# Attention queries and keys computed with tokens on the partitions instead of channels, in a two-layer transformer block on one core

## What is computed

```python
proj = jnp.einsum('bsd,de->bse', x, w_in)          # 2048 -> q, k, v, gate (2048 each), f_logit (16)
q = rms_norm(heads(q), q_gain)                     # 16 heads of 128; mean square over the head's 128
k = rms_norm(heads(k), k_gain)
c = jnp.cumsum(log_sigmoid(f_logit + b_f), axis=1) # per head and token
s = einsum('bhqd,bhkd->bhqk', q, k) * 128 ** -0.5 + c[query] - c[key]
p = softmax(where(key_pos <= q_pos, s, -inf))
y = (p @ v) * silu(gate);   out = y @ w_out
```

## Time and profile before

| | us |
|---|---|
| three runs: lowest, median, highest | 2485.38, 2486.83, 2490.3 |
| the profiled execution: its own time | 2487.29 |
| its span in the profile | 2485.4 |
| TensorE busy | 2411.2 (97%) |
| VectorE busy | 1700.3 (68%) |
| ScalarE busy | 1257.2 (51%) |
| GpSimd busy | 560.0 (23%) |

### The profile page before, as it was taken

How to read it: one execution, slowest core, us unless ns; L and a number is a source line. 1 busy time by engine, 2 the same in 40 slices (tenths; PEclk the granted TensorE clock), 3 DMA queues, 4 the chain that set the end, 5 groups by cost and what they waited for, 6 DMA issues and landing times.

```text
span 2485.4 us, 34202 instructions
## 1 busy us (share of the span) xinstructions
PE 2411.2 (97%) x13500; PEld 2079.5 (84%) x13500; DVE 1700.3 (68%) x2266; ACT 1257.2 (51%) x1780; POOL 560.0 (23%) x540
## 2 busy tenths in 40 slices
PE   7998999999999999999999999997999999999997
PEld 6777878888888888888788888886888888888886
DVE  7897578775566775577775766767666675666676
ACT  6767455444344444465555655635444444444444
POOL 4263154221013231152200000021221210221233
PEclk9999999999999999999999999999999999999998
DMA  7444646665565665556456555554565666555652
GB/s 241 145 135 153 224 153 188 187 191 182 190 198 188 188 188 179 184 170 194 143 158 180 157 170 170 152 172 135 160 190 178 189 181 197 163 189 178 190 178 94
DMA packets 126673, 434.90 MB, mean 175 GB/s; under 512 B 13489, under 2 KB 21041, under 8 KB 126513
## 3 DMA queue, kind: packets, MB, share of 16 engines
q1 hardware_dynamic: 126512, 432.72, 56.3%
HBM read 430.57 MB, written 2.10 MB: 174 GB/s over the span
## 4 chain that ended last, share of the span: by engine, by line
PE 88%; DVE 6%; ACT 3%; POOL 2%; issue 1%; DMA 0%; ACTq 0%; SPq 0%; POOLq 0%; DVEq 0%
PE bank L586 87%; DVE wlo L1251 2%; DVE S L1251 1%; ACT whi L874 1%; POOL hT L1805 1%; POOL acc L1805 1%; DVE hT L1254 1%; DVE ev L1264 0%; DVE ev L1254 0%; DVE S L1254 0%; ACT hT L1182 0%; PE bank L794 0%; ACT L1081 0%; DMA hT<-in_xT 0%; DVE xa L1254 0%
## 5 line engine op out<-in xcount | busy, mean ns | idle before, releaser
L1251 DVE TENSOR_TENSOR wlo<-raw,whi 128x1024 fp32r<-128x1024 f32 (+1 forms) x820 | 1026.0, 1258 | 672.1 <-ACT whi L874 670.1
L586 PE MATMUL bank<-xa,whi 128*128 128x512 f32 (+1 forms) x3968 | 1254.0, 398 | 24.5 <-DVE wlo L1251 11.4
L874 ACT ACTIVATE whi<-raw 128x1024 fp32r<-128x1024 f32 (+1 forms) x822 | 847.3, 1040 | 780.9 <-PE bank L586 775.5
L586 PEld LDWEIGHTS bank<-xa,wlo 128*128 128x128 f32 x3904 | 737.7, 189 | 173.0
L586 PE MATMUL bank<-xa,wlo 128*128 128x256 f32 x3904 | 773.8, 279 | 0.0
L586 PEld LDWEIGHTS bank<-xa,whi 128*128 128x128 f32 x3968 | 609.9, 189 | 39.5 <-DVE wlo L1251 16.1
L586 PE MATMUL bank<-xb,whi 128*128 128x512 f32 (+1 forms) x1948 | 571.4, 378 | 2.4 <-ACT S L1055 2.4
L586 PEld LDWEIGHTS bank<-xb,wlo 128*128 128x128 f32 x1776 | 336.0, 189 | 71.6
L586 PE MATMUL bank<-xb,wlo 128*128 128x256 f32 x1776 | 365.3, 279 | 0.0
L586 PEld LDWEIGHTS bank<-xb,whi 128*128 128x128 f32 x1948 | 300.5, 190 | 3.7 <-issue 3.0
L586 PE MATMUL bank<-whi,xa 128*128 128x512 f32 x768 | 245.0, 401 | 15.1 <-DVE wlo L1251 7.6
(11 more groups left out here) (193 smaller groups left out, 1379.4 us busy)
## 6 DMA issues: line engine op xcount, KB each, us to landing
raw<-in_w SPq DMA_DIRECT2D x792, 512.0 KB, 3.7
raw<-in_w SPq DMA_DIRECT2D x29, 256.0 KB, 2.7
hT<-in_xT SPq DMA_DIRECT2D x4, 512.0 KB, 7.5
hT<-in_xT SPq DMA_DIRECT2D x1, 2048.0 KB, 9.9
out<-hT SPq DMA_DIRECT2D x4, 512.0 KB, 3.0
X<-in_dec SPq DMA_DIRECT2D x8, 192.0 KB, 3.8
con<-in_con SPq DMA_DIRECT2D x1, 768.0 KB, 12.0
hT<-in_rcnt SPq DMA_DIRECT2D x1, 512.0 KB, 5.6
```

The lines of the kernel that those rows point to most:

```text
L586: return pe.matmul(o, w, x, start=start, stop=stop, skip_group_check=True)
L874: act.activation(hi, r, ACT.Copy).then_inc(*w_high(i))
L1251: return dve.tensor_tensor(o, x, y, op)
```

## The change

q and k become natural blocks of 512 columns (four heads at once). Their squares are taken by ScalarE straight from the bank and summed by VectorE along the free axis. After root and reciprocal, VectorE scales the tile while emptying it, four heads in one instruction, into `qkn`; TensorE transposes it to channels on partitions, eight transpositions for q and eight for k per group, and ScalarE copies the result out, k with the gains. `fq_total` and `fk_total` are gone. The forget row is no longer spread into a bank of its own and copied: the same product, now 384 columns wide, is accumulated onto the scores, and `soft` loses two of its four wide instructions. The order of blocks changes to fv, gates(0), fq, fk, gates(2) for the first three groups and fq, gates(0), fk, fv, gates(2) for the last. Heads are scored at e+4, e+5, e+7 and e+8 after the one `fk` block of the group.

The core of the diff (layout, then TensorE, ScalarE, VectorE):

```diff
+        def normed(w, col):
+            e = block(w, g, xa3, "fox_w_in", col + 512 * g, nat, "natural", 512)
+            late(e + 1, w + "_norm", g)
+            late(e + 3, w + "_turn", g)
+            return e
+        def heads(e, attend):
+            for i, (n, late_by) in enumerate(zip((4, 5, 7, 8), attend)):
+                for step in ("scores", "soft", "soft_exp", "soft_scale", "turn_p"):
+                    late(e + n, step, 4 * g + i)
+                    n += 1
+                late(e + n + late_by, "attend", 4 * g + i)
+                late(e + n + late_by + 1, "attend_split", 4 * g + i)
+        if g < 3:
+            values()
...
             gates(0)
+            normed("fq", 0)
+            heads(normed("fk", D), (0, 0, 0, 0))
+        else:
+            normed("fq", 0)
             gates(0)
-        for i in (0, 2):
-            e = block("fq", (g, i), xa3, "fox_w_in", 512 * g + 128 * i, full)
-            late(e + 1, "fq_total", g, i)
-            late(e + 2, "fq_norm", g, i)
-            e = block("fk", (g, i), xa3, "fox_w_in", D + 512 * g + 128 * i, full)
-            late(e + 1, "fk_total", g, i)
-            late(e + 2, "fk_norm", g, i)
...
+            heads(normed("fk", D), (0, 0, 2, 2))
+            values()
+        gates(2)
```

```diff
+                    elif step in ("fq_turn", "fk_turn"):
...
+                        for t in range(2):
+                            q.wait_ge(*vec_evac.of("tile", tile_of[w, g] + t))
+                        for i in range(4):
                             for t in range(2):
-                                m = mm(bank[6 + j][:, t:t + 1], sq[:, j, 128 * t:128 * t + 128], ones[:, 0:1], True, True)
+                                o = 256 * (i % 2) + 128 * t
+                                m = pe.transpose(bank[6 + i // 2][:, o:o + 128], qkn[w][:, t, 128 * i:128 * i + 128], ident)
...
-                            mm(bank[4 + j][:, 0:T], ones, sq[:, j, :], True, True).then_inc(*side("fk_total", g, i + j))
...
-                        mm(bank[6][:, 0:256], hot[:, h:h + 1].broadcast_to((48, 128)), rows[:, 0:256], True,
-                           True).then_inc(*side("forget_row", h))
+                        mm(B[:, 128:384], q_t[i][:, 128:256], k_t[i][:, :], False)
+                        mm(B[:, 0:384], hot[:, h:h + 1].broadcast_to((48, 128)), rows[:, 0:384], False,
+                           True).then_inc(*side("scores", h))
```

```diff
+                    elif step in ("fq", "fk"):
...
+                            act.activation(qk_sq[t], bank[n % 4][:, :], ACT.Square).then_inc(*squares(step, g, t))
+                    elif step in ("fq_norm", "fk_norm"):
...
+                        act.activation(qk_f[w], qk_f[w], ACT.Sqrt, scale=1.0 if w == "fq" else 1.0 / 128,
+                                       bias=eps128 if w == "fq" else eps6).then_inc(*act_val(w + "_norm", g))
+                    elif step in ("fq_turn", "fk_turn"):
...
+                            act.activation(qk_t[w][:, 512 * i:512 * i + 512], bank[6 + i][:, :], ACT.Copy,
+                                           scale=gains if w == "fk" else 1.0).then_inc(*act_evac(w + "_turn", g, i))
```

```diff
+                            dve.tensor_reduce(qk_f[step][:, 4 * t:4 * t + 4],
+                                              qk_sq[t].rearrange("p (h c) -> p h c", h=4), AX,
+                                              ALU.add).then_inc(*vec_val(step + "_sum", g, t))
...
+                            tt(qkn[w][:, t, :].rearrange("p (h c) -> p h c", h=4),
+                               bank[n % 4][:, :].rearrange("p (h c) -> p h c", h=4), f,
+                               ALU.mult).then_inc(*vec_evac("tile", n))
...
-                        stt(p[:, 0:128], B[:, 0:128], f[:, 0:1], r[:, 0:128], ALU.mult,
-                            ALU.add).then_inc(*vec_val("soft_half", h))
-                        stt(p[:, 128:384], B[:, 128:384], f[:, 1:2], r[:, 0:256], ALU.mult,
-                            ALU.add).then_inc(*vec_val("soft_in", h))
```

More of the change, by code:

```diff
@@ L259, in gates, with values @@
             late(e + 1, "fgate_silu", g, i)
-        if g:
-            gates(0)
[L262 to L266, removed]
-            gates(0)
-        if g < 3:
-            gates(2)
-        for i in (0, 2):
-            e = block("fq", (g, i), xa3, "fox_w_in", 512 * g + 128 * i, full)
-            late(e + 1, "fq_total", g, i)
-            late(e + 2, "fq_norm", g, i)
-            e = block("fk", (g, i), xa3, "fox_w_in", D + 512 * g + 128 * i, full)
-            late(e + 1, "fk_total", g, i)
-            late(e + 2, "fk_norm", g, i)
[L277 to L281, removed]
+        def values():
+            block("fv", g, xa3, "fox_w_in", 2 * D + 512 * g, nat, "natural", 512)
+        def normed(w, col):
[12 more added lines that the diff above has]
+            values()
+            if g == 0:
+                e = block("forget", 0, xa3, "fox_w_in", 4 * D, [(0, 16)], "stacked", cols=16)
+                late(e + 1, "forget_turn")
+                late(e + 3, "forget_sums")
+            gates(0)
+            normed("fq", 0)
+            heads(normed("fk", D), (0, 0, 0, 0))
+        else:
+            normed("fq", 0)
+            gates(0)
+            heads(normed("fk", D), (0, 0, 2, 2))
+            values()
+        gates(2)
     ends["fox"] = len(uses) - 1
@@ L791, in tensor_program @@
                         q.wait_ge(*vec_val.of("soft", h))
-                        q.wait_ge(*(act_evac.of("turn_p", h - 1) if h % 4 else act_evac.of("fq_norm", h // 4, 3)))
+                        q.wait_ge(*(act_evac.of("turn_p", h - 1) if h % 4 else act_evac.of("fk_turn", h // 4, 1)))
                         for n in range(3):
@@ L799, in tensor_program @@
                         q.wait_ge(*act_evac.of("turn_p", h))
[L800 to L803, removed]
+                        q.wait_ge(*act_evac.of("tile", tile_of["fv", h // 4] + 1))
+                        q.wait_ge(*(vec_val.of("attended", h - 1) if h % 4 else act_evac.of("fk_turn", h // 4, 0)))
                         mm(bank[6][:, 0:256], v_t[:, 0, c], PT[w][:, 0:256], True)
@@ L1085, in scalar_program @@
                         q.wait_ge(*vec_val.of("forget_row"))
[L1086 to L1112, removed]
-                            q.wait_ge(*side.of("fk_total", g, i + j))
-                            if i:
-                                q.wait_ge(*vec_val.of("fk", g, j))
-                            elif g:
-                                q.wait_ge(*vec_val.of("fk", g - 1, 2 + j))
-                            act.activation(rr[j], bank[4 + j][:, 0:T], ACT.Sqrt, scale=1.0 / 128,
-                                           bias=eps6).then_inc(*act_evac("fk_norm", g, i + j))
-                    elif step == "scores":
-                        h, = k
-                        q.wait_ge(*side.of("forget_row", h))
-                        if h >= 2:
-                            q.wait_ge(*side.of("attend", h - 2))
-                        act.activation(PT[h % 2][:, 0:T], bank[6][:, 0:T], ACT.Copy).then_inc(*act_evac("forget_row", h))
@@ L1166, in scalar_program @@
                             elif i >= KT - 2:
[L1167 removed]
+                                q.wait_ge(*(pool_val.of("ret_square", 7, 2 + j) if l else vec_val.of("fk_sum", 3, 0)))
                                 q.wait_ge(*vec_evac.of("last", l, i))
```

124 lines of the change are left out of this document (65 added, 59 removed).

## The result

| | before | after |
|---|---|---|
| median of five executions, us | 2486.83 | 2474.52 |
| lowest and highest | 2485.38, 2490.3 | 2474.42, 2477.4 |
| span in the profile | 2485.4 | 2472.6 |

The ratio is 0.9951, 95% interval 0.9937 to 0.9966: 12.3 us less, where 10.6 were forecast (2476.2, range 2473 to 2482.5).

What follows compares the result with a forecast made beforehand. The prediction took fox to be bound by TensorE's own instructions; -4.3 - 14.0 + 6.8 + 0.9 = -10.6 us from the median of 2486.83 gave 2476.2, with a range of 2473 to 2482.5.

Steps and rivals of the forecast that it cites:

- The bound: In fox, TensorE's own instructions set the time; work taken from VectorE or ScalarE pays nothing.
- Natural for turned, -4.3: q and k blocks in fox: natural steps of 0.680 replace turned ones of 0.697, 4.3 us less, bounds 0 and -4.3.
- rival 4: q and k blocks: the natural form gains nothing, so the sum is -6.3 and the time 2480.5; chance 0.07.
- Sums of squares, -14.0: Column sums for q and k leave TensorE, each insertion also delaying products behind it: 7.1 + 6.9, 14.0 us less.
- Transpositions, +6.8: 64 new transpositions of q and k on TensorE at a spacing of 0.107 each: 6.8 us more, bounds 5.1 and 17.7.
- The forget row, +0.9: Row product in fox of 384 columns instead of 256, 0.057 more, 16 times: 0.9 us more, bounds 0 and 2.7.
- New waits, "equal to the 0.7 that go": TensorE's new waits, tightest at the third head's `turn_p`, equal the 0.7 us that go; bounds 0.7 less, 1.5 more.
- 2 us of slack: At `fq_turn` and `fk_turn`, the scaled tiles take 5.6 to 6 us and TensorE arrives after 8.2.
- the groups' 98.7: Expected us between the same steps of neighbouring groups in fox, against 101.34 before.
- rivals 2 and 3: At `turn_p`: head 2 a piece late per group, 2487, chance 0.07; heads 2 and 3 both, 2498, chance 0.05.

Runs made afterwards that it cites:

- run 9: Changed kernel with each of VectorE's 16 sums of squares and 16 scaled evictions issued twice: median 2475.87 us, fox stretch 435.8.
- run 2: Kernel before without TensorE's sums over squares for q and k (output not the program's): fox stretch 12.6 us shorter, median 12.3 below the kernel before beside it.
- run 5: Changed kernel with the forget row again in its own bank, copied by ScalarE and added by VectorE: median 2474.49 us, fox stretch 434.4.
- run 1: The kernel before, unchanged, profiled once more: 2486.39 us (one execution), fox stretch 446.9 again, start of fox at 1218.50 instead of 1219.40.
- run 8: Changed kernel with a group's heads scored at e+4, e+5, e+6 and e+7 instead of e+4, e+5, e+7 and e+8: median 2476.85 us, fox stretch 438.1.
- run 7: Changed kernel with fox's forget-row operands on 128 partitions, zero from 48 up, instead of 48: median 2467.39 us, fox stretch 429.0.
- run 10: Kernel before with fox's forget-row operands on 128 partitions instead of 48: median 2481.37 us, fox stretch 443.1.

## Why the prediction was right

**The bound.** Right. TensorE was busy for 89 of 89 us in both kernels, its busy time fell by what the time fell, and 22 us added to VectorE changed nothing (run 9).

**Natural for turned, -4.3.** Right in kind, a little too large. Away from insertions the step in q and k is 0.680, as read from the values' block, so rival 4 is out. But the first steps behind an insertion or a turned block take 0.69 or 0.70. Over all natural steps of fox that do not directly touch an insertion the mean is 0.683, over the turned ones 0.697: 256 times 0.0137 is 3.5. The five steps of the earlier trace rows were all of the quiet kind. No run had this term alone.

**Sums of squares, -14.0.** Right. Taken out alone they gave 12.6 (run 2), because 1.2 came back as waits for VectorE that the changed kernel does not have.

**Transpositions, +6.8.** Measured 7.0 and 7.2. The choice of the spacing, read from three transpositions, over the duration, was what the sign of the whole forecast hung on.

**The forget row, +0.9.** By its rows 0.06 a head, 1.0 in all, as forecast; putting it back gave 1.4 of the stretch (run 5).

**New waits, "equal to the 0.7 that go".** This is the step that was off: there are none. At the group's third head I counted a chain of 5.7 to 6.1 us on ScalarE and VectorE against 6.2 on TensorE. The timeline of the changed kernel shows it, from `turn_p` of head 1 over the next split to the small reciprocal of head 2, and TensorE's arrival:

```profile
1303.91 0.49 PE L802 MATMUL bank<-con,X 128*128 128x128 f32 x3
...
1305.71 1.05 ACT L880 ACTIVATE whi<-raw 128x1024 fp32r<-128x1024 f32 x1
...
1306.66 0.40 ACT L1140 ACTIVATE xb<-S 128x256 fp32r<-128x256 f32 x1
...
1308.60 0.15 DVE L1638 RECIPROCAL sm<-sm 128x2 f32<-128x2 f32 x1
...
1310.41 0.49 PE L802 MATMUL bank<-con,X 128*128 128x128 f32 x3
```

From 1303.91 to the reciprocal at 1308.60 and the two instructions of `soft_scale` behind it, which end at 1309.34, the chain takes 5.4, and TensorE comes at 1310.41, 6.5 after the start; 1.1 us are left. I had added durations, but neighbours on ScalarE and VectorE start before the one ahead has ended in the record: 1.05 us of split are followed by the next instruction after 0.95. The same holds for the turn itself, where I gave 2 us of slack and q has 3.2 (the scaled evictions end at 1352.99):

```profile
1351.70 1.29 DVE L1249 TENSOR_TENSOR S<-bank,sm 128x512 f32<-128x512 f32 x2
...
1356.23 1.04 PE L780 MATMUL bank<-con,S 128*128 128x128 f32 x8
```

The waits that went were also worth more than the 0.7 of the earlier trace rows. The list counts only the time after the end of the product ahead, and the record of that product, 0.39 long, runs on past the 0.23 after which the next one usually starts. Before, at one of the three places:

```profile
1415.70 0.39 PE L586 MATMUL bank<-wlo,xa 128*128 128x512 f32 x1
1416.34 0.55 PE L794 MATMUL bank<-con,X 128*128 128x128 f32 x3 [0.25 <-DVE X L1257]
1416.64 0.70 PE L586 MATMUL bank<-whi,xa 128*128 128x512 f32 x2
```

The three transpositions start 0.64 after the last product of the stream instead of 0.23, and take 0.30 instead of 0.24: 0.47 lost, where the list has 0.25. With the two others like it and 0.31 in the last group, which the list leaves out, that is 1.7.

So the forecast of 10.6 came near 11.1 partly by luck: the natural form was put 0.8 too high, and the waits, set equal, in truth gave 1.7. With the measured terms, -3.5 - 14.0 + 7.0 + 1.0 - 1.7 = -11.2, against 11.1 in the stretch. That the groups' 98.7 was measured as 98.54 rests on the same two errors. The median's further microsecond lies ahead of fox and is scatter of the kind that run 1 and run 9 show.

**Slower by late heads (rivals 2 and 3).** VectorE's list is what runs late first, as they said, but not at the step that they named and not at their price: with one piece less (run 8) TensorE lost 0.4 us a group at `attend`, not a piece at `turn_p`.

## What to carry to other kernels

Where TensorE is busy without a break, price a change by the starts of its neighbours in the timeline, not by durations or by busy sums of other engines: the distance to the next start, and how much later than usual the one after that comes. Price a wait in the same way: 0.64 instead of 0.23 to the next start is a loss of 0.41, where the list of waits counts the idle time of 0.25 alone. An order of steps has a slack of its own beside its count of instructions, and a saving on TensorE is only worth what this slack can follow (the same edit gave 3.8 us in one order and 6.8 in the other). And look at loads of the stationary operand that sit behind idle time without a releaser.

## What the runs showed of the hardware that I had not expected

A product over 48 partitions amid products over 128 costs about 0.4 us more than the same product over 128 partitions with zeros (run 7; run 10 shows it in the kernel before), 0.27 of it ahead of the product and 0.12 behind. Its own duration is the smaller one, 0.43 against 0.52, so it looks the cheaper of the two in any list of durations. I had priced the row product by its columns and had not looked at the starts around it, which show it in the kernel before as well. Sixteen float32 transpositions in a row keep a spacing of 0.10 to 0.11 us and leave the products behind them at their usual spacing.
